# One-core fp32 model kernel: a new normed x enters k by k over eight products instead of four, GpSimd sums the squares, and three stage ends are reordered

## What is computed

```
def rmsnorm(x, g):
    var = jnp.mean(xf * xf, axis=-1, keepdims=True)
    return (xf * lax.rsqrt(var + RMS_EPS) * g)
for i in range(2):                                     # first model
    uz = einsum(rmsnorm(x, g_pre[i]), w_in[i])         # feeds "window" (i=0), "conv" (i=1)
    u, z = uz[..., :4096], uz[..., 4096:]
    y = pool_mixer(u, ...) if i == 0 else rglru(causal_depthwise_conv(u, ...), ...)
    o = einsum(y * silu(z), w_out[i])                  # "squared"
    x = x + rmsnorm(o, g_post[i])
    gate = sigmoid(einsum(rmsnorm(x, g_ple_in[i]), w_ple_gate[i]))   # feeds "gate"
    x = x + rmsnorm((p[i] @ w_ple[i]) * gate, g_ple_out[i])          # p @ w_ple: "plain"
for l in range(2):                                     # second model
    proj = rms_norm(x, norm_g) @ w_in[l]               # feeds "gqk" and the stages after it
    ...                                                # latent attention, spatial gate, gated linear attention
    x = x + merged @ w_out[l]                          # "wo"
```

## Time and profile before

| | us |
|---|---|
| median of 3 runs | 3455.66 (3449.29 to 3475.31) |
| the profiled execution | 3467.84, of it 3466.0 span |
| PE busy | 3385.7 (98%) |
| DVE busy | 2280.0 (66%) |
| ACT busy | 1663.6 (48%) |
| POOL busy | 910.2 (26%) |

### The profile page before, as it was taken

One profiled execution on the slowest core, in us unless ns is written; L12 is line 12 of the kernel. 1 busy time (PEld: TensorE's weight loads), 2 busy tenths in 40 slices (PEclk: granted clock), 3 DMA queues, 4 the chain that ended last, 5 costly groups with the idle time before them and its releaser, 6 DMA issues.

```text
span 3466.0 us, 67608 instructions
## 1 busy us (share of the span) xinstructions
PE 3385.7 (98%) x28796; PEld 3368.9 (97%) x28796; DVE 2280.0 (66%) x3038; ACT 1663.6 (48%) x2090; POOL 910.2 (26%) x895
## 2 busy tenths in 40 slices
PE   8999999989999999989999999999999999999999
PEld 8999999989999999989999999999999999999999
DVE  7866654668888745667867755555667777555554
ACT  4334444554488644545544444444455444444443
POOL 4832310034556400203513300000016233100000
PEclk9999999999999999999999999999999999999999
DMA  6655665455655655545444456566554444555555
GB/s 219 197 179 194 194 219 196 150 158 199 197 180 183 208 194 172 175 151 175 142 156 144 147 195 195 192 196 193 190 173 144 159 134 147 187 185 187 188 185 171
DMA packets 168780, 619.31 MB, mean 179 GB/s; under 512 B 18720, under 2 KB 19360, under 8 KB 168096
## 3 DMA queue, kind: packets, MB, share of 16 engines
q1 hardware_dynamic: 165888, 602.23, 53.3%
q10 hardware_dynamic: 2592, 12.75, 1.0%
HBM read 610.71 MB, written 4.19 MB: 177 GB/s over the span
## 4 chain that ended last, share of the span: by engine, by line
PE 85%; DVE 7%; ACT 4%; POOL 2%; issue 1%; DMA 0%; ACTq 0%; POOLq 0%; SPq 0%; DVEq 0%
PE banks L517 25%; PE banks L509 25%; PE banks L510 24%; DVE w_lo L1193 3%; ACT w_hi L846 2%; PE pm L556 1%; PE pm L557 1%; PE pm L561 1%; POOL win L1877 1%; PE pm L517 1%; PE pm L510 1%; PE pm L509 1%; PE ms_bank L538 1%; PE pm L610 1%; DVE wide L1215 1%
## 5 line engine op out<-in xcount | busy, mean ns | idle before, releaser
L1193 DVE TENSOR_TENSOR w_lo<-raw,w_hi 128x1024 fp32r<-128x1024 f32 x1144 | 1456.0, 1276 | 936.5 <-ACT w_hi L846 914.2
L846 ACT ACTIVATE w_hi<-raw 128x1024 fp32r<-128x1024 f32 x1144 | 1203.1, 1057 | 1015.6 <-PE banks L517 929.0
L509 PE MATMUL banks<-xs,w_hi 128*128 128x256 f32 x5320 | 1265.1, 279 | 0.6 <-ACT w_hi L846 0.6
L510 PE MATMUL banks<-xs,w_hi 128*128 128x256 f32 x5320 | 1263.2, 279 | 0.0
L509 PEld LDWEIGHTS banks<-xs,w_hi 128*128 128x128 f32 x5320 | 1007.6, 189 | 1.2 <-ACT w_hi L846 1.0
L510 PEld LDWEIGHTS banks<-xs,w_hi 128*128 128x128 f32 x5320 | 1007.6, 189 | 0.2
L517 PE MATMUL banks<-xs,w_lo 128*128 128x256 f32 x5320 | 739.6, 281 | 2.5 <-DVE w_lo L1193 2.5
L517 PEld LDWEIGHTS banks<-xs,w_lo 128*128 128x128 f32 x5320 | 668.7, 190 | 3.9 <-DVE w_lo L1193 3.1
L509 PE MATMUL banks<-inner,w_hi 128*128 128x256 f32 x1280 | 301.5, 277 | 0.0
L510 PE MATMUL banks<-inner,w_hi 128*128 128x256 f32 x1280 | 301.4, 277 | 0.0
L509 PEld LDWEIGHTS banks<-inner,w_hi 128*128 128x128 f32 x1280 | 241.0, 188 | 0.0
(11 more groups left out here) (323 smaller groups left out, 4897.4 us busy)
## 6 DMA issues: line engine op xcount, KB each, us to landing
raw<-weights SPq DMA_DIRECT2D x1144, 512.0 KB, 3.4
wide<-x_in ACTq DMA_DIRECT2D x4, 512.0 KB, 8.9
wide<-x_in ACTq DMA_DIRECT2D x1, 2048.0 KB, 7.7
x_scratch<-wide ACTq DMA_DIRECT2D x1, 2048.0 KB, 10.2
wide<-x_scratch ACTq DMA_DIRECT2D x1, 2048.0 KB, 7.8
out_x<-wide SPq DMA_DIRECT2D x3, 512.0 KB, 6.0
w_st<-w_s ACTq DMA_DIRECT2D x2, 512.0 KB, 4.2
b_st<-b_s ACTq DMA_DIRECT2D x2, 512.0 KB, 5.6
```

Source lines behind the costliest of these rows:

```text
L509: nc.tensor.matmul(bank, w_hi[:, slot, w], x[:, 0:T], start=(k + t == 0), stop=False)
L510: nc.tensor.matmul(bank, w_hi[:, slot, w], x[:, T:2 * T], start=False, stop=False)
L846: nc.scalar.activation(w_hi[:, slot, :], raw[:, slot, :], ACT.Copy).then_inc(hi_done, 1)
L1193: nc.vector.tensor_tensor(w_lo[:, slot, :], raw[:, slot, :], w_hi[:, slot, :].bitcast(F32), ALU.subtract).then_inc(lo_done, 1)
```

## The change

- A fed stage's first 16 units (turns 0 and 1, eight products) run over k outside and eight products inside: one tile of k a unit. The eight lie two to a bank, in the halves of banks 2, 3, 5 and 6 (`WIDE_BANKS`); later products take seven banks in the order of `NEXT_BANKS`. In the `layer 1` `squared` stage still four products run by rows. The stream of weights on the host is reordered to match.
- The eight are read when all are done: in `window`, `conv` and `gate` turns 2 and 3 read one product in each of their 16 units (turn 2 those of turns 0 and 1, turn 3 those of turns 2 and 3); in `gqk` all eight are read behind the last unit. Later turns are as before.
- For f < 5 ACT writes the first block of squares into `sq_sum`, POOL adds the other three and folds it in half (`sum_squares`, three adds of 128x1024 and one of 128x512), and PE multiplies two tiles after unit 13. The root and the reciprocal stand behind unit 14's split.
- Ends: `window`'s last two products are split inside `pooled` and `win` lies elsewhere; at the end of `plain` the first two tiles of xs are made ahead of the update of the next two; `squared` has seven banks and begins at bank 0. In the feeds, splits stand ahead of `hi_tiles` and `lows`.

```diff
--- before.py
+++ after.py
...
+WIDE_BANKS = (2, 3, 5, 6)
+NEXT_BANKS = (0, 1, 4, 2, 3, 5, 6)
...
-        if self.by_rows and i == 0 and j < 3:
-            return BANKS + j
-        return (self.bank0 + j) % self.n_banks
+        if self.fed and i < 2:
+            return WIDE_BANKS[j]
+        if self.fed:
+            return NEXT_BANKS[((i - 2) * self.width + j) % ALL_BANKS]
+        return (self.bank0 + i * self.width + j) % self.n_banks
...
-        win, inv_count = place("win", 64, [P, 6, PAD + T]), place("inv_count", 71, [P, 4, T])
+        win, inv_count = place("win", 96, [P, 6, PAD + T]), place("inv_count", 103, [P, 4, T])
...
-            s.n_banks = {"lru": LRU_BANKS, "plain": ALL_BANKS}.get(name, BANKS)
+            s.n_banks = {"lru": LRU_BANKS, "squared": ALL_BANKS, "plain": ALL_BANKS}.get(name, BANKS)
...
-            bank0 = 0 if s.name in ("lru", "plain") else bank0
+            bank0 = 0 if s.name in ("lru", "squared", "plain") else bank0
...
+            if s.fed and i < 2:
+                return s.mark0 + 2 * len(s.marks)
...
+            if s.name == "gqk":
+                return [divmod(m, 4) for m in range(8)] if i == 1 and u == s.units - 1 else []
+            if s.fed and i < 4:
+                return [] if i < 2 else [divmod(8 * (i - 2) + u, 4)]
             if s.by_rows and i == 0:
                 return [(0, 0)] if u == s.units - 1 else []
             if s.by_rows and i == 1 and u < 3:
                 return [(0, u + 1)]
-            if s.fed and i == 1 and u < 5:
-                return [(1, u - 3)]
-            return [(i, j) for j, p in enumerate(s.products)
-                    if p.last_unit == u and not (s.fed and i == 1 and j < 2)]
+            return [(i, j) for j, p in enumerate(s.products) if p.last_unit == u]
...
-            def square_block(l, which, f, b):
-                pe.wait_ge(x_sq, f * 4 + b + 1)
-                if b == 0:
-                    wait(pe, root_ready, norms[l, which])
-                for j in range(4):
-                    ins = nc.tensor.matmul(ms_bank[:, 0:T], mean_d[:, :], (act if b % 2 else val)[:, j, :],
-                                           start=(b == j == 0), stop=(b == j == 3))
-                ins.then_inc(ms_ready if b == 3 else sq_used, 1)
...
+                width = 8 if s.fed else 4
+                for u in range(s.units * width // 4):
                     slot = (s.unit0 + u) % SLOTS
-                    tile_of = [divmod(u * UNIT_TILES + c, 4) for c in range(UNIT_TILES)]
+                    tile_of = [divmod(u * UNIT_TILES + c, width) for c in range(UNIT_TILES)]
                     pe.wait_ge(hi_done, s.unit0 + u + 1)
                     for c, (k, j) in enumerate(tile_of):
                         if j == 0:
                             ready(k)
-                        bank, w = product_bank(s, 0, j), slice(c * P, (c + 1) * P)
-                        nc.tensor.matmul(bank, w_hi[:, slot, w], operand[:, k, 0:T], start=(k == 0), stop=False)
-                        nc.tensor.matmul(bank, w_hi[:, slot, w], operand[:, k, T:2 * T], start=False, stop=False)
+                        bank, w = product_bank(s, j // 4, j % 4), slice(c * P, (c + 1) * P)
+                        nc.tensor.matmul(bank, w_hi[:, slot, w], operand[:, k, 0:T], start=(k == 0 and j < 4),
+                                         stop=False, skip_group_check=True)
+                        nc.tensor.matmul(bank, w_hi[:, slot, w], operand[:, k, T:2 * T], start=False, stop=False,
+                                         skip_group_check=True)
...
-                def squares_between(u):
-                    if f < 5 and u in (2, 4, 6):
-                        square_block(s.layer, which, f, u // 2 - 1)
-                first_turn(s, xs, lambda k: pe.wait_ge(xs_ready, f * ND + k + 1), squares_between)
-                if f < 5:
-                    square_block(s.layer, which, f, 3)
-                else:
-                    pe.wait_ge(sq_summed, 1)
-                    mean_square(s.layer, which, [sq_sum[:, j, :] for j in range(4)])
+                def mean_of_x(u):
+                    if u == 13:
+                        pe.wait_ge(sq_summed, f + 1)
+                        mean_square(s.layer, which, [sq_sum[:, j, :] for j in range(4 if f == 5 else 2)])
+                first_turn(s, xs, lambda k: pe.wait_ge(xs_ready, f * ND + k + 1), mean_of_x)
...
+                dest = sq_sum if f < 5 and b == 0 else act if b % 2 else val
+                nc.scalar.activation(dest[:, :, :], x_buf[:, 4 * b:4 * b + 4, :], ACT.Square)\
...
+                    split(0)
                     squares(f, 0)
+                    split(1)
+                    split(2)
                     hi_tiles(f, gain, 3)
-                    split(0)
+                    split(3)
                     squares(f, 1)
-                    split(1)
+                    split(4)
                     hi_tiles(f, gain, 4)
-                    split(2)
+                    split(5)
+                    squares(f, 2)
+                    split(6)
                     hi_tiles(f, gain, 5)
+                    split(7)
                 else:
                     hi_tiles(f, gain, 5)
-                    for u in range(3):
+                    for u in range(4):
                         split(u)
-                squares(f, 2)
-                split(3)
-                split(4)
+                    squares(f, 2)
+                    for u in range(4, 8):
+                        split(u)
                 squares(f, 3)
-                for u in range(5, s.units):
+                for u in range(8, 2 * s.units):
                     split(u)
+                    if u == 14:
+                        root(s.layer, "ple" if s.name == "gate" else "enter")
...
+                        if s.name == "plain" and u == 2:
+                            hi_tiles(feeds, f"g_ple_in{l}", 0)
+                            hi_tiles(feeds, f"g_ple_in{l}", 1)
                         if s.name == "plain" and u == 3:
-                            for c in range(3):
-                                hi_tiles(feeds, f"g_ple_in{l}", c)
+                            hi_tiles(feeds, f"g_ple_in{l}", 2)
...
                else:
                     if s.name != "gate":
                         update(f, 0)
+                        lows(f, gain, 0)
                         update(f, 1)
-                        lows(f, gain, 0)
                         lows(f, gain, 1)
                         update(f, 2)
                         lows(f, gain, 2)
+                    split(0)
                     update(f, 3)
-                    split(0)
+                    split(1)
+                    split(2)
                     lows(f, gain, 3)
-                    split(1)
                     update(f, 4)
+                    split(3)
+                    split(4)
                     lows(f, gain, 4)
-                    split(2)
                     update(f, 5)
-                    split(3)
-                if f in (0, 5):
-                    if f == 0:
-                        lows(f, gain, 5)
-                    split(3)
-                else:
+                    split(5)
+                    split(6)
                     lows(f, gain, 5)
-                for u in range(4, s.units):
+                for u in range(7, 2 * s.units):
                     split(u)
+                    if u == 14:
+                        norm(s.layer, "ple" if s.name == "gate" else "enter", rstd_x)
...
+                        if s.name == "pooled" and i == 0 and u in (3, 5):
+                            window_split(window_rest.pop(0))
...
-                            for c in range(3):
-                                update(feeds, c)
+                            update(feeds, 0)
+                            update(feeds, 1)
+                            lows(feeds, f"g_ple_in{l}", 0)
+                            lows(feeds, f"g_ple_in{l}", 1)
+                        if s.name == "plain" and u == 2:
+                            update(feeds, 2)
                         if s.name == "plain" and u == 3:
-                            for c in range(3):
-                                lows(feeds, f"g_ple_in{l}", c)
+                            lows(feeds, f"g_ple_in{l}", 2)
...
+            def sum_squares(f):
+                for b in range(1, 4):
+                    gp.wait_ge(x_sq, f * 4 + b + 1)
+                    ins = nc.gpsimd.tensor_tensor(sq_sum, sq_sum, (act if b % 2 else val)[:, :, :], ALU.add)
+                    if b < 3:
+                        ins.then_inc(sq_used, 1)
+                        gp.wait_ge(sq_used, f * 2 + b)
+                link(ins)
+                nc.gpsimd.tensor_tensor(sq_sum[:, 0:2, :], sq_sum[:, 0:2, :], sq_sum[:, 2:4, :], ALU.add)\
+                    .then_inc(sq_summed, 1)
...
-    def first_by_rows(w):
-        return [w[:4].transpose(1, 0, 2, 3), w[4:]]
+    def first_by_rows(w, n=8):
```

(12 more changed lines are left out.)

57 lines of the change are left out of this document (34 added, 23 removed).

## The result

| | before | changed |
|---|---|---|
| median of 20 runs each, us | 3455.74 | 3437.6 (3418.87 to 3454.16) |
| ratio | | 0.9942 [0.9927, 0.9958] |
| span of the profiled execution | 3466.0 | 3445.3 |
| PE busy | 3385.7 | 3354.9 |
| DVE busy | 2280.0 | 2310.9 |

The changed kernel takes 0.58% less, 20 us by the ratio, and 20.7 us less between the two profiled spans. A 24.5 us gain and 3431 us were forecast. The changed kernel, run again unaltered beside other runs of the kernel before (experiment 9), gave 3430.81 us and a ratio of 0.9892 [0.9823, 0.9961].

A forecast was written before the change was run, and what follows sets the result against it. PE, busy 98% of the span, bounds the kernel: 1144 units of weights at its pace plus interruptions. Gains of 10.0 + 7.4 + 0.7 + 3.4 + 2.1 + 0.9 = 24.5 us give 3431 us on the median (chance 0.47), range 3406 to 3457.

The forecast's parts named there:

- Squares: In five feeds, four blocks of squares leave PE and two tiles come: 5.4 us a feed, all on PE's path.
- Feed: First 16 units of fed stages: waits for xs go, with the clock they cost; first gqk takes 47.4 us, 10.0 gained.
- Plain's end: End of plain: xs tiles come earlier, bank 6 behind ACT's copy is late next; 2.5 us gained.
- The debt of the gates: Gate's readings loop at 3.43 us against PE's 2.72; PE waits 10 us at the end; 3.7 gained twice with plain's end.
- Conv: In conv, DVE's 3.93 us loop gives 11.8 us of waits, against squares and feed waits saved: 0.7 us gained.
- Window: Window and pooled: squares and pooled's w_lo wait with its clock give 11.8, POOL's reading loop costs 8.4; 3.4 us gained.
- Lru to squared: Squared behind lru: three units already split run in the 7.2 us gap, leaving a 5.5 us pause; 2.1 us gained.
- Loops that don't bind: Rival: the reading loops in gate, conv and window overlap more and cost nothing: 3391 us, chance 0.10.
- The feeds still wait: Rival: each feed but the first still loses 2 us twice, with the clock behind it: 3447 us, chance 0.12.
- Adds at their worst: Rival: each POOL add holds DVE its whole 2.47 us, five feeds 0.9 us longer: 3436 us, chance 0.05.
- Faster pace: Rival: the second mix falls into PE's faster pace, 15.4 us less: 3416 us, chance 0.17.
- the slower pace spreads: Rival: pooled, silu and squared (+17 us) and the first mix (+15.4) fall into PE's slow pace: 3463 us, chance 0.09.

The follow-up runs named there:

- experiment 9: The changed kernel run again unaltered, beside other runs of the kernel before: 3430.81 us, ratio 0.9892.
- experiment 2: Changed kernel with 14 more mean_d matmuls ahead of each norm of x in the first five feeds, putting the squares' time back on PE: 3465.39 us, ratio 1.0029.
- experiment 6: Changed kernel with four products in every feed's first turn, old banks and split order, squares still summed on POOL: 3465.07 us, ratio 1.0005 to the kernel before.
- experiment 1: Changed kernel with DVE in gate reading a product ahead of the unit's w_lo: 3417.22 us, ratio 0.9899; again on another chip 3414.41 us, 0.9859.
- experiment 3: Changed kernel with POOL's three 128x1024 adds in each of the first five feeds cut to one element a partition: 3435.07 us, ratio 0.9933.
- experiment 4: Changed kernel with conv alone back to four products in its first turn, old splits and banks, squares still over POOL: 3438.49 us, ratio 0.994.
- experiment 5: Changed kernel with the end of plain put back, tiles 0 to 3 updated first and their xs made afterwards: 3452.7 us, ratio 0.9958.

## Why the prediction was right, and where it was off

*The forecast itself.* 3437.6 us against 3431. Its mechanism stands: waits for `xs` go, five to six microseconds a feed of squares go, and a part is given back where the products are read. But it was not the case given 0.47 as it was written. One of its three signs of being wrong was "if the mix stages change their pace", and the last mix did, 407.04 to 391.68 us. That the profiled span came out near the forecast even so is luck: the gain there was nearly eaten by `pooled`, `silu` and `squared` at the other pace.

*Squares, 5.4 us a feed on PE's path*: right, 5.8 (experiment 2). The sentence hid a condition: it holds for the wide feed alone. In the narrow one, with POOL adding in their place, it gives nothing (1.0005, experiment 6); all but `window` take 5 to 9 us more.

*Feed.* The first `gqk` was forecast at 47.4 us and took 47.4; in `gate` the 16 units took 47.7 and 45.9, where the sum had 45.2 (44.3 and 0.9 for the clock) and 46.0 at most.

*Plain's end*: 2.5 forecast, 2.0 and 1.8 measured, 2.4 when undone. Bank 6 and ACT's copy were the next thing, as said.

*The debt of the gates*: PE idle 10 us ahead of the norm was forecast, 10.7 and 11.0 measured, the loop at 3.42 us as in the earlier trace rows; experiment 1 takes it away. *Mis-sized*: "3.7 us gained, twice", 7.4 for both ends and gates, was 1.8. (By its own times, 758.21 less 754.6, it is 3.6; and the 1.6 us within the stage are 42.6 less 40.8, 1.8, which nothing else hangs on.) From their 17th unit to the next stage both gates took 62.6 us, and the sum had 61.8 (754.6 less 692.8): 0.8 more each, a small part. The plain ends bring 1.3 less together, and the two feeds are 2.5 and 0.7 us longer than the sum. Against that, the second `plain` and `gate` had been 0.7 us longer than the first before the change, which "twice" left out. The windows over the feeds show next to no wait, but a lower clock in the first:

```profile
662.34:710.03 47.69, 47.69 (x389) 47.58 (x390) 42.65 (x42) 26.39 (x35) 13.78 (x5) 0.96 0.56 188
1383.80:1429.69 45.89, 45.69 (x389) 45.38 (x390) 42.19 (x41) 26.40 (x35) 15.03 (x5) 1.00 0.62 195
```

The first pays the whole 1.7 us that the sum had as an upper bound for the clock behind the pause, and took 0.9 of; the rest is PE's second pace, which the sum left out although had it: 365 of its 389 matmuls followed at about 118 ns and not 113 (1.6 us), 212 of 389 in the second.

*Conv*: 0.7 forecast, 1.4 measured: 10.6 gained in the feed (9.5 forecast), 9.2 given back behind it (8.8). Waits for `w_lo` and a bank are 9.9 us, where 11.8 was the sum:

```profile
PE pm L524 <- DVE w_lo L1200: 3.6, 4, 0.9
PE banks L524 <- DVE w_lo L1200: 3.5, 4, 0.9
PE banks L516 <- DVE taps_in L1627: 1.7, 1, 1.7
PE banks L561 <- DVE w_lo L1200: 1.1, 1, 1.1
```

*Window, 3.4 us gained*: off, -0.5. The feed gained the 5.4 of the squares and the rest of the stage lost 7.5, less than the 8.4 of the sum. What failed is the end: `pooled`, forecast to gain 6.4 by losing its wait, gained 1.6. It still waits 1.4 us for `w_lo`, in two waits, and it ran at the lower pace: 3.0 of its 92.0 us are that, by the 89.0 of experiment 1. With the pace out, 2.5 are gained.

*Lru to squared*: right, net 2.1, with a pause of 4.5 us where 5.5 was given.

*Rivals.* Loops that don't bind: no. The feeds still wait: no, in the changed kernel PE waits for `xs` only at the start of a stage. Adds at their worst: not on PE's path, experiment 3 finds 1.7 us in a feed at most. On DVE itself it is another matter: single adds cost more than the earlier trace rows showed. The rule that was weighed, from the Trainium skill, SBUF — State Buffer, section Who interferes with whom, is that the two exclude each other for the whole instruction. The trace agrees: four tiles of `xs` that began 0.06 us behind an add of 2.35 us took 2.1 us more (experiment 4), and in the `conv` of the changed kernel (experiment 3) the adds waited for DVE in the same way. Faster pace and slower pace both happened at once: the last mix fell into the faster one and gave 18.8 us with its `wo`; `silu` and `squared` fell into the slower and took 13.7, and `pooled` 3.0, together the 17 us that the rival "the slower pace spreads" had for these three.

*What stays open* is what picks PE's pace. `silu` and the first `squared` were slow in both profiles of the changed kernel and in experiment 2, fast in the one before and in eight others; a mix was slow only in the profile before and in experiment 5. Where `silu` was slow, most of `pooled` ahead of it was slow too (678 to 724 of its 768 matmuls), and in the nine others at most 47 were: the pace looks as if it were carried over from stage to stage. The program alone does not fix it: the two runs of experiment 1 had 103 and 912 slow matmuls in `conv`, 364 and 1919 (of 1920) in `lru`. No run was made to change that alone. It costs 22 to 30 us in the two profiles of experiment 1, where it was 40.6 and 39.9 in the two of the changed kernel; in stages that another engine paces it costs nothing (the gates' second halves took 62.6 us with 0 and with 1.7 us of it). So of the 42.1 us that separate the spans of experiment 1 and the changed kernel, 19.4 are the gates, 16.7 are `pooled`, `silu` and `squared` at the other pace, and 4.9 lie between the first `gqk` and the first mix, which no edit touched.

*The whole in one line*: the wide feed with the squares' time on PE loses some 10 us (experiment 2), POOL's sums in narrow feeds gain nothing (experiment 6), and both together gain 20: POOL's adds need the slack of the wide feed, and the wide feed pays only with PE rid of the squares.

## What to carry to other kernels

Work on the bound engine that stands in its own waiting time is not on its path: before it is moved to another engine, ask who there works beside it, and whether the feed has slack for that. Where a stage reads one result per step, put the reading ahead of the operation that waits for this step's input; a loop over three engines is cut by the order on one. Try each part of a change alone: here a kernel with one of the two main parts undone was in each case no faster than the one before, and with both the gain is 0.6%, and the order of two instructions took another 19 us from the two gates.

## What the runs showed of the chip that was not expected

PE has two paces at full clock: 144 units in 391.68 or 407.04 us, 64 in 174.08 or 180.91, with PEclk at 1.00 in both and PE busy throughout. In all twelve profiles `silu`, the first `squared` and both mixes ran from end to end at one of them, and a slow `silu` always stood behind a slow `pooled`. DVE's operations with two inputs in SBUF and a POOL add exclude each other, and the one that begins first keeps its time: four tiles took 3.77 us for 1.69 under an add of 2.35 (experiment 4), and an add that began 0.01 us behind three `w_lo` of 3.49 us took 5.74 (experiment 3).
